# A two-layer streaming encoder step on eight cores: the kernel rewritten with tokens phase by phase, a block convolution in column tiles, norms by token tile, attention rows with a maximum, and four weight slots

## What is computed

```python
for i in range(2):
    mod = silu(c) @ w_mod[i] + b_mod[i]                  # 6 vectors of 2048 per sequence
    sh1, sc1, g1, sh2, sc2, g2 = split(mod, 6)
    h = rms_norm(x, norm_mix[i]) * (1 + sc1) + sh1
    if i == 0:
        a, gt = split(h @ w_pw1 + b_pw1, 2)              # 2048 -> 4096
        u = a * sigmoid(gt)
        z = causal_depthwise_conv(u, w_dw, width=31) + b_dw
        y = silu(layer_norm(z)) @ w_pw2 + b_pw2
    else:                                                # 32 query heads, 4 key heads, head_dim 64
        q, k, v = h @ w_qkv + b_qkv                      # frame in chunk c reads chunks c-2, c-1, c
        s = q k^T / 8 + rel_bias
        y = softmax([s, sink])[:-1] v @ w_o + b_o
    x = x + g1 * y
    h = rms_norm(x, norm_ffn[i]) * (1 + sc2) + sh2
    g, u = split(h @ w_gu[i], 2)                         # 2048 -> 2 * 5632
    x = x + g2 * ((silu(g) * u) @ w_down[i])
y = rms_norm(x, norm_out)
```

## Time and profile before

| | us |
|---|---|
| time, median of 3 runs (4203.78 to 4612.38) | 4582.28 |
| span of the profiled execution, slowest core | 4205.1 |
| spans of the eight cores in it | 4189.3 to 4205.1 |
| PE busy | 3540.9 (84%) |
| ACT busy | 1266.4 (30%) |
| DVE busy | 1179.3 (28%) |
| POOL busy | 175.5 (4%) |

### The profile page before, as it was taken

One profiled execution on the slowest core, in us unless ns is written; L12 is line 12 of the kernel. 1 busy time (PEld: TensorE's weight loads), 2 busy tenths in 40 slices (PEclk: granted clock), 3 DMA queues, 4 the chain that ended last, 5 costly groups with the idle time before them and its releaser, 6 DMA issues.

```text
span 4205.1 us, 60541 instructions; the slowest of 8 cores (4189.3 to 4205.1 us)
## 1 busy us (share of the span) xinstructions
PE 3540.9 (84%) x23856; PEld 2001.7 (48%) x23856; DVE 1179.3 (28%) x2198; ACT 1266.4 (30%) x2784; POOL 175.5 (4%) x332
## 2 busy tenths in 40 slices
PE   1199879777799999999985698898959999999983
PEld 0155445533355555555542376333636656565551
DVE  0211276632221212121212300554231121212224
ACT  2211144434322212121215311676342231312223
POOL 0000000000000000000000000000000000000000
PEclk9599989889899999999998797555979999999996
DMA  7856544012355555546463132000413433434332
GB/s 162 135 103 124 102 81 79 3 31 51 67 100 106 96 109 92 112 90 115 86 113 53 23 58 41 1 1 2 79 22 60 81 67 70 74 61 81 61 56 88
DMA packets 66709, 308.65 MB, mean 73 GB/s; under 512 B 19936, under 2 KB 20928, under 8 KB 37504
## 3 DMA queue, kind: packets, MB, share of 16 engines
q0 software_dynamic: 51840, 283.78, 37.2%
q1 hardware_dynamic: 14592, 21.01, 1.7%
HBM read 579.03 MB, written 10.17 MB: 140 GB/s over the span
## 4 chain that ended last, share of the span: by engine, by line
PE 72%; ACT 12%; DVE 8%; DMA 3%; issue 3%; SPq 1%; ACTq 0%; DVEq 0%; POOL 0%; POOLq 0%
PE ps L207 72%; ACT SCR L210 8%; DVE X L411 4%; ACT HBraw L210 3%; DMA RING<-wmod 2%; SPq L202 1%; DVE HBraw L644 1%; DVE HBraw L641 1%; DVE SCR L375 1%; DMA yT<-SCR 0%; DMA SCR<-wdwT 0%; ACT L210 0%; DVE SCR L993 0%; DVE HBraw L861 0%; ACTq L81 0%
## 5 line engine op out<-in xcount | busy, mean ns | idle before, releaser
L207 PE MATMUL ps<-HBraw,RING 128*128 128x352 bf16 (+5 forms) x11136 | 1782.8, 324 | 167.5 <-ACT HBraw L210 166.2
L207 PEld LDWEIGHTS ps<-HBraw,RING 128*128 128x128 bf16 (+1 forms) x11136 | 1034.9, 98 | 904.3 <-issue 178.7
L207 PE MATMUL ps<-UBraw,RING 128*128 128x352 bf16 (+2 forms) x5760 | 981.0, 324 | 137.0 <-ACT SCR L210 97.1
L207 PEld LDWEIGHTS ps<-UBraw,RING 128*128 128x128 bf16 x5760 | 517.3, 98 | 600.1 <-issue 271.3
L411 DVE TENSOR_TENSOR X<-X,SCR 128x352 f32<-128x352 f32 (+2 forms) x672 | 368.3, 548 | 740.6 <-ACT SCR L210 740.6
L210 ACT ACTIVATE SCR<-ps,MOD 128x16 f32<-128x16 f32 (+4 forms) x960 | 389.4, 448 | 510.6 <-DVE X L411 309.4
L210 ACT ACTIVATE SCR<-ps 128x352 f32<-128x352 f32 (+2 forms) x264 | 127.5, 483 | 1199.6 <-PE ps L207 1199.6
L468 DVE TENSOR_TENSOR UBraw<-ps,SCR 128x352 bf16<-128x352 f32 (+2 forms) x264 | 144.5, 547 | 1186.1 <-PE ps L207 1186.1
L207 PE MATMUL ps<-UBraw,SCR 128*128 128x384 bf16 (+3 forms) x2272 | 369.4, 304 | 89.5 <-DVE MOD L331 56.3
L207 PEld LDWEIGHTS ps<-UBraw,SCR 128*128 128x128 bf16 (+1 forms) x2272 | 191.6, 99 | 273.2 <-issue 176.2
L210 ACT ACTIVATE HBraw<-HBraw 128x256 bf16<-128x256 f32 (+6 forms) x496 | 185.2, 403 | 130.3 <-DVE HBraw L861 101.7
(11 more groups left out here) (67 smaller groups left out, 1148.8 us busy)
## 6 DMA issues: line engine op xcount, KB each, us to landing
RING<-wmod POOLq DMA_DIRECT2D x96, 1024.0 KB, 8.8
RING<-wgu POOLq DMA_DIRECT2D x88, 1024.0 KB, 8.9
RING<-wdn POOLq DMA_DIRECT2D x80, 512.0 KB, 5.5
RING<-wpw POOLq DMA_DIRECT2D x24, 1024.0 KB, 14.0
RING<-wqkv POOLq DMA_DIRECT2D x10, 1024.0 KB, 8.7
X<-xT SPq DMA_DIRECT2D x4, 2368.0 KB, 42.5
yT<-SCR SPq DMA_DIRECT2D x16, 528.0 KB, 2.7
RING<-wo POOLq DMA_DIRECT2D x8, 1024.0 KB, 8.7
```

Source lines behind the costliest of these rows:

```text
L207: return PE.emit(nc.tensor.matmul(out, lhsT=lhsT, rhs=rhs, start=start, stop=stop, **kw))
```

## The change

The kernel is written anew; inputs, outputs and the split over cores stay. Tokens of each tile lie phase by phase: of 384 tokens first those whose number is 0 modulo 4, then 1, 2 and 3 (the host reorders inputs and outputs).

- **Ring**: four slots; a block's transfer is issued when its slot is released (`advance`). The down projection has blocks of 512 columns, 4 a group.
- **Modulation**: the weights are now the moving operand; 8 matmuls of 512 columns a block into four column tiles, 8 blocks a vector, then four DVE transposes. The 96 blocks are spread as 16 at the start, 24 in the pointwise convolution, 56 in the first feed-forward layer.
- **Convolution**: after each chunk's pointwise part four DMAs move its four phases to 32 partitions each (L624). Four neighbouring channels by four phases then make blocks; a chunk is 34 slots x 4 column tiles, each a matmul of 312 columns with a 128 x 32 matrix. z goes to X; the sums for the layer norm are made in three column tiles. The layer norm comes after all chunks, by token tile, beside the first six output blocks of the projection; X is then fetched again from HBM.
- **Norms**: squares and sums are made as each block of X is finished, for three token tiles apart; the last two blocks of a projection (and the last down group) run tile by tile, and the norm is applied to a tile under the next tile's matmuls.
- **Down projection**: one DVE instruction multiplies out of PSUM and adds to X; a group's down part follows the next group's first gate/up block.
- **Attention**: queries in partitions (two heads' 64 rows a step), 66 steps. DVE adds the bias (from the host) out of PSUM and takes the maximum, ACT takes the exponential with its sum, GpSimd multiplies by 1/sum, PE transposes by products with the identity. Seven of the eight query blocks are interleaved, 12 matmuls a step.

```diff
+            for k2 in range(2):
+                k = 2 * part + k2
+                for j in range(4):
+                    mm(bank[32 * j:32 * j + 32, :], SCT[:, k, :], wv[:, k2, j, :], k == 0, k == KC - 1,
+                       tile_position=(0, 32 * j))
...
+            for po in range(4):
...
+                for i, (b, s) in enumerate(CSLOTS[po]):
+                    for g in range(4):
+                        mm(PS[bi][32 * g:32 * g + 32, 0:312], dgv[:, NSLOT * g + s, :], upv[:, g, 8 + b:320 + b], i == 0, i == last,
+                           tile_position=(0, 32 * g))
+                ACT.wait(PE.tick())
...
-            DVE.emit(nc.vector.tensor_tensor(out=DG[:, b, 0:NDV, :], in0=IDB[:].unsqueeze(1).to_broadcast([128, NDV, 128]),
-                                             in1=WDW[:, 0:NDV, c:c + 1].to_broadcast([128, NDV, 128]), op=ALU.mult))
...
-            for w in range(31):
-                mm(bank[:, 0:384], DG[:, b, w, :], UB[:, c, zlo + 2 + w:zlo + 2 + w + 384], w == 0, w == 30)
...
+                    mm(PS[bi][32 * t:32 * t + 32, 0:416], ONESB[:, 0:32], src[:, c % 2, TS[t]:TS[t] + 416], c == 0, c == KC - 1,
+                       tile_position=(0, 32 * t))
...
+                rl_t[c] = dma(SP, UP[32 * ph:32 * ph + 32, c % 2, :].rearrange("p (g b) -> p g b", b=NBLK), u[:, ph, :], rl_sem[c % 2])
...
+                    tt(X[:, c, cols], X[:, c, cols], MEAN[:, t % 2, 0:n], ALU.subtract)
+                    tk[c] = DVE.tick()
+                if c >= 1:
+                    p = c - 1
+                    DVE.wait(tk[p])
+                    tt(X[:, p, cols], X[:, p, cols], RSC[:, t % 2, 0:n], ALU.mult)
+                    ACT.wait(DVE.tick())
+                    act(HB[:, p, 32 + TS[t]:32 + TS[t] + n], X[:, p, cols], AF.Silu, scale=vcol("lng", p), bias=vcol("lnb", p))
...
+                        x_tok[(t, p // 4)] = dma(SP, X[:, p - 3:p + 1, cols], xr[:, p - 3:p + 1, 32 + TS[t]:32 + TS[t] + n],
+                                                 xr_sem[4 * t + p // 4])
...
+                for jj in range(GSIZE[G]):
+                    mm(PS[bi][:, 0:N], w[:, jj, 128 * h:128 * h + 128], ACTR[:, (G % 2) * 8 + jj, o:o + N], jj == 0, jj == GSIZE[G] - 1)
+                tp = PE.tick()
+                DVE.wait(tp)
+                xx = xv(n, lay, t, True)
+                stt(xx, cv3(PS[bi][:, 0:P_], lay, t), MOD[:, li, 80 + n, 0:1], xx, ALU.mult, ALU.add)
...
+                    mm(PS[bi][:, lo:lo + n], w[:, k, 128 * h:128 * h + 128], rhs_of(k, t), k == 0, k == KC - 1)
...
+                held.append((n, t, resid(bi, li, lay, n, t, tp, xtok_of(n, t))))
+                if len(held) > 1:
...
+                if gen is not None:
+                    pump(gen, 5)
...
+                        if t > 0 and b == 0 and h == 2:
+                            nm.done[t - 1] = True
+                            norm_finish(nm, t - 1)
+                            gen = nm.apply(nm, t - 1)
+                        if gen is not None:
+                            pump(gen, 2)
...
+                DVE.emit(nc.vector.tensor_copy(out=sk, in_=vcol("sinkp", sc).to_broadcast([128, 2])))
...
+                tt(out, sv, bias, ALU.add)
...
+                DVE.emit(nc.vector.tensor_reduce(out=NM[:, r, :], in_=SS[:, r, :].rearrange("p (j k) -> p j k", j=2)[:, :, 0:nk + 1],
+                                                 axis=mybir.AxisListType.X, op=ALU.max, negate=True))
...
+                    o, nk = (193 * j, 193) if kind == "p" else (193 * j, 145)
+                    act(SS[:, r, o:o + nk], SS[:, r, o:o + nk], AF.Exp, bias=NM[:, r, j:j + 1], accum_out=DEN[:, r, j:j + 1])
...
+                DVE.wait(exp_tok[(s, h)])
+                DVE.emit(nc.vector.reciprocal(out=DEN[:, r, :], in_=DEN[:, r, :]))
+                POOL.wait(DVE.tick(), tr_tok.get(s - 1))
...
+                    POOL.emit(nc.gpsimd.tensor_scalar_mul(out=PB[:, h, po:po + nk], in0=SS[:, r, o:o + nk], scalar1=DEN[:, r, j:j + 1]))
...
+                for (o, m, d) in cols:
+                    mm(PS[4 + h][0:m, 128 * d:128 * d + 128], PB[:, h, o:o + m], IDB[:], True, True)
...
+                    if kind == "p":
+                        mm(out[:, 0:256], VT[:, i + v, gc], PT[:, h, 256 * v:256 * v + 256], v == 0, v == 1, tile_position=(0, 64 * h))
...
+            DVE.emit(nc.vector.tensor_copy(out=QT[:, o:o + 256], in_=PS[bi][:, 0:256]))
...
+        for s in range(NSTEP + 2):
+            if s < NSTEP:
+                s_mm(s)
+            if 1 <= s <= NSTEP:
+                s_norm(s - 1)
+            if s < NSTEP:
+                s_ttr(s)
+                s_exp(s)
+            pump(qg, 4)
+            if s >= 2:
+                pv_mm(s - 2)
+            pump(qg, 4)
+            if 1 <= s <= NSTEP:
+                t_mm(s - 1)
+                pt_copy(s - 1, 0)
+                pt_copy(s - 1, 1)
+            pump(qg, 4)
+            if s >= 2:
+                o_copy(s - 2)
```

More of the change, by code:

```diff
@@ L228, in build_nc, with tt @@
[L228 to L239 removed]
+        def tt(out, in0, in1, op):
+            return DVE.emit(nc.vector.tensor_tensor(out=out, in0=in0, in1=in1, op=op))
@@ new lines, in build_nc, with mods0 @@
+        nb_done = 0
+        def mods0(n):
+            nonlocal nb_done
+            order = list(range(8, 16)) + list(range(8))
+            for b in order[nb_done:nb_done + n]:
+                mod_block(0, b, 7)
+            nb_done += n
+        DVE.wait(t_c)
+        DVE.emit(nc.vector.tensor_copy(out=IDB[:], in_=MT[:]))
+        DVE.emit(nc.vector.tensor_copy(out=ID32[:], in_=MT[:, 0:32]))
+        for j in range(1, 4):
+            sync(DVE)
+            tt(ID32[:], ID32[:], MT[:, 32 * j:32 * j + 32], ALU.add)
@@ new lines, in build_nc @@
+        ACT.wait(sqf[1])
+        for ti, (a, b_) in enumerate(tiles0):
+            act(RSTD0[:, a:b_], PS[ti][:, 0:b_ - a], AF.Sqrt, bias=EPSC[:, 0:1], scale=1.0 / D)
+            bank_tok[ti] = [ACT.tick()]
+        DVE.wait(ACT.tick())
+        DVE.emit(nc.vector.reciprocal(out=RSTD0, in_=RSTD0))
+        sync(DVE)
+        tt(XP, XP, RSTD0[:, 0:32].unsqueeze(1).to_broadcast([128, KC, 32]), ALU.mult)
+        for c in range(KC):
+            tt(X[:, c, :], X[:, c, :], RSTD0[:, 32:NH], ALU.mult)
@@ new lines, in build_nc @@
+        sync(DVE)
+        tt(LST[q96, 1, :], LST[q96, 0, :], LST[q96, 0, :], ALU.mult)
+        sync(DVE)
+        stt(LST[q96, 1, :], PS[6][q96, 0:416], 1.0 / D, LST[q96, 1, :], ALU.mult, ALU.subtract)
+        t_s = DVE.tick()
+        bank_tok[5] = [t_s]
+        bank_tok[6] = [t_s]
+        ACT.wait(t_s)
+        act(LST[q96, 1, :], LST[q96, 1, :], AF.Sqrt, bias=EPSC[q96, 0:1], scale=1.0)
+        DVE.wait(ACT.tick())
+        DVE.emit(nc.vector.reciprocal(out=LST[q96, 1, :], in_=LST[q96, 1, :]))
@@ new lines, in build_nc @@
+        pump(genN, 4)
+        kv_group(0, 0, 0)
+        pump(genN, 4)
+        kv_group(0, 1, 0)
+        pump(genN, 4)
+        kv_group(1, 0, 0)
+        pump(genN, 40)
+        kv_group(1, 1, 0)
+        for which in range(2):
+            for gp in range(2):
+                kv_group(which, gp, 1)
+        for which in (1, 0):
+            for gp in range(2):
+                t_kv = kv_group(which, gp, 2)
+        ring.release("kv_k", PE.tick())
+        ring.release("kv_v", PE.tick())
+        steps, bsq = [], []
@@ new lines, in pt_copy @@
+        def pt_copy(s, h):
+            kind = steps[s][0]
+            e = ACT if h == 0 or s % 2 == 0 else DVE
+            e.wait(tr_tok[(s, h)], pv_tok.get(s - 1))
+            for (rows, lo, hi) in ([(128, 0, 512)] if kind == "p" else [(128, 0, 256), (16, 256, 512)]):
+                if e is ACT:
+                    act(PT[0:rows, h, lo:hi], PS[4 + h][0:rows, lo:hi], AF.Identity)
+                else:
+                    DVE.emit(nc.vector.tensor_copy(out=PT[0:rows, h, lo:hi], in_=PS[4 + h][0:rows, lo:hi]))
+            bank_tok[4 + h] = [e.tick()]
+            pt_tok[(s, h)] = e.tick()
```

1877 lines of the change are left out of this document (1040 added, 837 removed).

## The result

The changed kernel takes 3491.65 us (four runs, 3491.06 to 3493.11). Against the kernel before this is a ratio of 0.827 (95% interval 0.822 to 0.832), so faster by 17%. The forecast was 3300, its range 3170 to 3690: the time lies inside the range and 192 us above the forecast. The profiled execution spans 3490.8 us.

What follows compares the result with a forecast made beforehand. Dense stages were taken as bound by PE's matmul columns, the rest by PE waiting as work passes to ACT and DVE. Savings 55 + 282 + 31 + 165 + 192 + 58 + 66 + 57 = 906; 4205 - 906 = 3299, so 3300 us, range 3170 to 3690.

Steps and rivals of the forecast that it cites:

- four rivals: Column tiles gain nothing, 3590 (0.07); attention at 6 us a step, 3380 (0.15); less clock, 3680 (0.20); tile-change drains, 4305 (0.03).
- Convolution: Pointwise and depthwise convolution: 675 to 393 us, with four column tiles side by side at 0.15 us a round.
- rule on weight loads: Convolution: loads overlap matmuls only across differing row groups, so 239 us, 157 more than taken; the prediction's rows disagreed.
- Start: Kernel start, before the pointwise convolution: 207 to 152 us, bounds 140 and 165.
- 12 x 6.2 = 74 gives 136: Start: after inputs arrive at 61.7 us, twelve remaining modulation blocks load at 6.2 us each, ending at 136.
- Layer norm: Layer norm, output projection and norm after the convolution: 199 to 168 us, bounds 145 and 195.
- 18 + 22 + 22: Layer norm: DVE leads, 17.9 us for a tile's subtractions and products, plus 8 residual additions of 0.56 for tiles 1 and 2.
- Feed-forward: Feed-forward 0 with its norm before and after: 1272 to 1107 us; feed-forward 1: 1021 to 955 us.
- so DVE keeps up: Down projection: one DVE evacuation of about 0.62 us against 1.3 us of matmuls.
- Attention: Keys, values, queries and attention: 571 to 379 us, with 66 steps at 4.8 us; bounds 250 and 400 for the steps.
- rival 2: Attention takes 6 us a step, from PE at 1.2 GHz or GpSimd at 1.5 us a product: 3380 us, chance 0.15.
- Clock: Dense stages keep a granted clock of 0.98 to 0.99; the opposing case, less clock, gives 3680 us, chance 0.20.

Runs made afterwards that it cites:

- the experiment: Changed kernel (3491.65 us) with the next tile's layer-norm steps queued ahead of the residual evacuations and the third tile's spread made earlier: 3464.8 to 3468.7 us.

## Why the prediction was right, and where its sum was wrong

**Direction and most of the gain: right.** 714 us were gained of 906 forecast. None of the four rivals came.

**Convolution: the mechanism right, the sum helped by terms that offset each other.** 0.139 us a round against 0.15, 16 x 4.73 = 76 us against 82. The 10 for the hand-over of banks does not show, since the 4.73 us of a chunk hold it; modulation took 24 x 0.54 = 13 against 19; statistics 16 x 0.53 = 8 against 6. Against this, PE waits some 32 us where the sum had 8: the last relayout 14.0, the others together 5 (1.2 and 2.5 the longest), and 13 for evacuations and transposes. The relayout lands in 13.6 us (median), not 11.3, and is covered but for that. The experiment with the tiles' order shows that the reason was right too, as the prediction put it, tiles "within reach of the queue". By the rule on weight loads in the Trainium skill (TensorE: Matmul & The Clock Gate, Part 3) the prediction had estimated 239 us; the trace does not agree, 76 us, and the measurement decides. The Trainium skill (TensorE: Matmul & The Clock Gate, Part 3) also states that the starts of a pack lie about 4 ns apart, and here the trace agrees: 3 ns in most records of a chunk.

**Start: 162 for 152.** "By the inputs' arrival 4 are loaded" was right: four transfers were issued at 1.56 and landed within 36 us. The step that failed is the next, "12 x 6.2 = 74 gives 136": it let the other twelve start at 61.7. The ring has four slots, and the next transfer is issued only when PE has released one.

```profile
66.80 2.19 PE L302 MATMUL ps<-SCR,ONESB 128*128 128x416 bf16 x6 [66.80 <-DVE BQ L463]
...
73.43 0.53 POOL L127 DMA_DIRECT2D RING<-wmod  x1 [69.61 <-PE ps L302]
...
152.50 1.05 PE L302 MATMUL ps<-RING,SCT 128*32 128x512 bf16 x8 [5.17 <-DMA RING<-wmod]
```

PE's first modulation block (71.82) stands in its queue behind the sums of squares of four chunks, and these begin at 66.80, when the last small inputs have come. From 65 to 75 us the DMA engines are 5% busy. The twelve blocks thus start 12 us late and take 79 us to the use of the last instead of 74; the application behind it takes 10 instead of 16. This is read from the trace, no run changed it.

**Layer norm: 229 for 168.** The step is the sum "18 + 22 + 22". It put each tile's layer norm beside the matmuls of the tile before, by the engines' durations. Those were no longer than priced (0.94 us a chunk on DVE against 1.12), but the order in ACT's queue put them one after the other; the waits of 16.8, 16.4 and 5.9 us are 39 of the 61. Another 14 are the five waits at the end, where the norm's application stands ahead of the last evacuations; the granted clock of 0.83 in this stage costs on top. The first part is shown by the experiment. The second is read from the trace only, and three steps of the application instead of five between evacuations left these waits as long in sum.

**Feed-forward: 1152 for 1107, 1016 for 955.** The step is "so DVE keeps up": it compared DVE's time with PE's over a block and did not ask when a bank comes free. In feed-forward 1 two banks cost 40 us of the 61, which is shown; in feed-forward 0 the group of four costs some 12 by its rows, of which three banks gave back 7. The rest is read from the trace only: the entrance, where gate/up matmuls wait for the norm's application (34 us for 17 us of matmuls in feed-forward 1, 52 for 33 in feed-forward 0, 4 of them a wait for weights), and 48 matmuls with ones at 0.16, which the sum left out. Modulation gave back 56 x 0.27 = 15. Attention's projection, 138 for 125, has four waits for the squares at its end, 10.6 us, which its sum left out.

**Attention: 376 for 379, a right number with a wrong reason, so luck.** 4.8 us a step was the middle between a busy DVE and PE at 1.2 GHz. PE ran at 0.96 of full speed while it had queries, DVE was busy for 3.2 us of a step, and the 4.64 us are a chain of waits through several queues. Neither rival 2 nor the forecast had this mechanism. Two errors also cancel: the steps took 305 us instead of 66 x 4.8 = 317, and what lies ahead of them 66 instead of 56. GpSimd's weight issues, costed at nothing, do stand on the chain (1.1 us where it was read).

**Clock: right.** The dense stages stand at 0.99, and four runs lie within 2 us. By the Trainium skill (TensorE: Matmul & The Clock Gate, Part 1) dense matmuls on three cores of a die bring that die to 13/16 of the clock; in these four runs this does not show, the mean granted clock of every core is 0.952 to 0.955.

The range took in the loss of its rivals, not of its terms: the forecast's own range, 3170 to 3450, was missed by 42 us, and the largest errors of the sum, in the start, the layer norm and the down projection, were waits in a queue or for a bank that it priced as covered.

## What to carry to other kernels

Where work is to lie beside other work, write down the order of the queue of each engine that both use, and look for an instruction ahead of it that waits for the other; durations alone said "covered" in the layer norm and the down projection, and it cost 39 and 40 us; in attention the orders held about 50. A wait in a loop over engines can be held by several queues at once: here reordering one moved nothing or made it worse, and one more step between front and back on all of them gave the gain, so take the chain of waits again after each edit. Count PSUM banks by the slowest evacuation, not by the mean.
